# Ending the gathered rows five units earlier, and moving LN2 of the gathered tiles forward

## The reference

```
z = x @ W_in                                   # q, k, v, conv B, C, h and two gates
m = (sigmoid(g_attn) * attention @ W_attn_out + sigmoid(g_conv) * conv @ W_conv_out) @ W_o
h = LN1(2**0.25 * x + m)
q = h @ w_q; per head: top 16 of 128 keys on both halves, top 16 of their 256 sums -> expert, gate
act = gelu(h . u_tab[expert]);  y = sum over 8*16 experts of gate * act * v_tab[expert]
out = LN2(2**0.25 * h + y)
```

## Time and profile before

| | us |
|---|---|
| median of three runs | 3909.4 (3905.04 to 3912.0) |
| the profiled execution | 3916.73 |
| its span, first to last instruction | 3914.9 |
| mean granted clock of PE | 0.985 of full speed |

### The profile page before, as it was taken

How to read it: one execution, slowest core, us unless ns; L and a number is a source line. 1 busy time by engine, 2 the same in 40 slices (tenths; PEclk the granted TensorE clock), 3 DMA queues, 4 the chain that set the end, 5 groups by cost and what they waited for, 6 DMA issues and landing times.

```text
span 3914.9 us, 60806 instructions
## 1 busy us (share of the span) xinstructions
PE 3766.4 (96%) x24471; PEld 3482.9 (89%) x24471; DVE 2720.5 (69%) x3355; ACT 1379.6 (35%) x1966; POOL 1096.0 (28%) x587
## 2 busy tenths in 40 slices
PE   8999999998999999999999889999998888999997
PEld 8999999998988888888888889999998877878785
DVE  4544555455788765566655577888887887888898
ACT  5544444443323100000000334566663333344342
POOL 0000000001634444344433532211113442334442
PEclk9999999999999999999999999999999999999998
DMA  5345555554689999999999449999999999999996
GB/s 186 109 155 182 182 182 182 184 183 169 241 346 384 409 421 399 405 391 408 394 393 391 169 144 354 364 374 376 360 360 396 409 409 376 409 400 393 393 410 243
DMA packets 209849, 1236.87 MB, mean 316 GB/s; under 512 B 20176, under 2 KB 53536, under 8 KB 66336
## 3 DMA queue, kind: packets, MB, share of 16 engines
q1 hardware_dynamic: 124448, 659.65, 44.3%
q0 software_dynamic: 73728, 536.90, 33.6%
q10 hardware_dynamic: 11520, 38.28, 2.4%
HBM read 1196.48 MB, written 37.75 MB: 315 GB/s over the span
## 4 chain that ended last, share of the span: by engine, by line
PE 82%; DMA 9%; DVE 7%; issue 1%; ACT 1%; SPq 0%; ACTq 0%; DVEq 0%
PE dense_ps L909 23%; PE dense_ps L898 13%; PE dense_ps L899 13%; PE dense_ps L900 13%; PE dense_ps L1151 6%; DMA wbuf<-in_peer_v_dram 4%; PE dense_ps L939 3%; PE score_ps L1151 3%; DMA row<-in_peer_v_dram,expert 3%; DVE h L1189 3%; DMA wbuf<-in_w_units_dram 2%; PE o_ps L1151 1%; PE oT_ps L1151 1%; PE score_ps L1108 1%; PE o_ps L1032 1%
## 5 line engine op out<-in xcount | busy, mean ns | idle before, releaser
L1235 DVE TENSOR_TENSOR w_lo<-wbuf,w_hi_r 128x1024 fp32r<-128x1024 f32 x808 | 982.3, 1222 | 575.5 <-ACT w_hi_r L554 575.0
L554 ACT ACTIVATE w_hi_r<-wbuf 128x1024 fp32r<-128x1024 f32 x872 | 915.4, 1059 | 1155.5 <-PE dense_ps L900 631.1
L898 PE MATMUL dense_ps<-act_hi,w_hi_r 128*128 128x256 f32 x4128 | 1185.3, 287 | 49.1 <-DVE w_lo L1235 42.2
L899 PE MATMUL dense_ps<-act_lo,w_hi_r 128*128 128x256 f32 x4128 | 1174.9, 285 | 0.0
L900 PE MATMUL dense_ps<-act_hi,w_lo 128*128 128x256 f32 x4128 | 1174.8, 285 | 0.0
L898 PEld LDWEIGHTS dense_ps<-act_hi,w_hi_r 128*128 128x128 f32 x4128 | 798.9, 194 | 59.8 <-DVE w_lo L1235 34.0
L505 POOL DMA_INDIRECT row<-in_peer_v_dram,expert x256 | 494.6, 1932 | 1127.5 <-DVE h L1189 1103.2
L899 PEld LDWEIGHTS dense_ps<-act_lo,w_hi_r 128*128 128x128 f32 x4128 | 799.0, 194 | 0.0
L900 PEld LDWEIGHTS dense_ps<-act_hi,w_lo 128*128 128x128 f32 x4128 | 798.4, 193 | 0.0
L909 PE MATMUL dense_ps<-xT,wbuf 128*128 128x256 f32 x3136 | 688.1, 380 | 0.8 <-ACT xT L539 0.8
L909 PEld LDWEIGHTS dense_ps<-xT,wbuf 128*128 128x128 f32 x3136 | 594.3, 190 | 86.2 <-issue 5.3
(11 more groups left out here) (220 smaller groups left out, 4214.2 us busy)
## 6 DMA issues: line engine op xcount, KB each, us to landing
wbuf<-in_w_units_dram SPq DMA_DIRECT2D x456, 1024.0 KB
wbuf<-in_peer_v_dram SPq DMA_DIRECT2D x128, 1024.0 KB
act_spill<-stage ACTq DMA_DIRECT2D x64, 256.0 KB, 8.8
gate_spill<-gbuf ACTq DMA_DIRECT2D x8, 2048.0 KB, 11.2
e_act<-act_spill SPq DMA_DIRECT2D x32, 512.0 KB, 10.7
e_gate<-gate_spill SPq DMA_DIRECT2D x32, 512.0 KB, 13.1
cT<-in_x_dram SPq DMA_DIRECT2D x2, 2048.0 KB, 11.3
row<-in_peer_u_dram,expert POOLq DMA_INDIRECT x256
```

Source lines behind the costliest of these rows:

```text
L554: act.activation(w_hi[:, j, :], wbuf[n % 2][:, j, :], ACT.Copy).then_inc(w_hi_ready, 1)
L898: nc.tensor.matmul(out, w[0], x[0], start=opens, stop=False)
L899: nc.tensor.matmul(out, w[0], x[1], start=False, stop=False)
L1235: V.tensor_tensor(w_lo[n % 2][:, j, :], wbuf[n % 2][:, j, :], w_hi[:, j, :].bitcast(F32), ALU.subtract).then_inc(lo_by_dve, 1)
```

## The change

Two numbers of `rows_in` and one line of constants:

```diff
-STATS_AT, SD_AT, APPLY_AT, OUT_AT = (19, 62), (21, 62), (24, 63), (27, 63)
+STATS_AT, SD_AT, APPLY_AT, OUT_AT = (3, 57), (5, 58), (7, 59), (9, 60)
...
     if m >= 0:
         left = ALL_ROWS - ROWS_TO[N_V - 1]
-        return left * min(m + 1, 62) // 62 - left * min(m, 62) // 62
+        return left * min(m + 1, 57) // 57 - left * min(m, 57) // 57
```

## The result

| | before | changed |
|---|---|---|
| median of 20 runs each, us | 3911.73 (3899.76 to 3921.22) | 3919.18 (3914.63 to 3929.91) |
| the profiled execution, us | 3916.73 | 3929.91 |
| its span, us | 3914.9 | 3928.1 |

The ratio is 1.0021 with a 95% interval of 1.0012 to 1.0030, so the change costs 7.5 us by the medians and 8.2 by the ratio (4.7 to 11.7). The profiled execution of the changed kernel is the slowest of its 20, 10.7 us above their median, and the one of the kernel before is 5.0 us above its own; what they show of sizes is read with that in mind.

The account below looks back on a forecast made before the run. It took PE and the nearly full transfers (412 GB/s) as level, with a serial VectorE tail at the end. Terms -6.1 + 0 + 4.2 + 0 - 1.1 = -3.0 us took 3909.4 to 3906.4; range 3897 to 3918.

Parts of the forecast that it names:

- signs of failing: PE ending over 12 us later or earlier at all, 2.52 and 4.71 us waits returning, or a new 5 us wait.
- The tail: At the kernel's end, VectorE starts the last piece at 3883.7 in place of 3889.81: -6.1 us.
- LN2 of tile 1 in its new place: In sections 57 to 59, its 4.7 us of passes fit into VectorE's free time: 0 us, up to +3 without cover.
- The five rows: By section 56, five more rows need 12.7 us of transfers, 3.5 MB in idle capacity: PE ends 4.2 us later.
- rival A: Second table's stage: free capacity is only echo, PE ends 12.7 us later; net +5.5 us, 3914.9; chance 0.20.
- LN2 of tile 0: Moved from sections 19 to 27 to sections 3 to 9: 0 us in sum, between -5 and +5.
- Units 57 to 63: The last units, without rows: the 1.12 us wait at 3833 goes, -1.1 us.

Follow-up runs that it names:

- rows57_ln1: The changed kernel with LN2 of tile 0 back in sections 19 to 27; ratio 1.0017 to the kernel before.
- rows60_ln1: The kernel before with rows ending at unit 59 and LN2 of tile 1 in sections 59 to 62; ratio 1.0003 to the kernel before.
- rows57_only: The kernel before with only the rows moved, ending at unit 56, LN2 of both tiles as before; ratio 1.0020 to the kernel before.
- half-row kernels: Kernel before, changed kernel, and changed kernel with LN2 of tile 0 in sections 19 to 27, each gathering 512 KB from row 408: 0.9908, 0.9904, 0.9893.
- ln0_early: The kernel before with only LN2 of tile 0 moved, to sections 3 to 9; ratio 0.9993 to the kernel before.
- before_half_take: The kernel before with VectorE adding only 1024 of a row's 2048 floats from row 408 on, transfers whole; ratio 0.9968, median 3903.86.

## Why the prediction was wrong

The forecast was 3.0 us faster and the change is 7.5 us slower; 3919.2 lies above the range of 3897 to 3918. Two of the prediction's own signs of failing came: PE's stage was 20.5 us longer in the profile, where 12 was the limit, and the wait of 6.75 us stands before unit 13.

*The tail, -6.1 us:* right to the tenth of a microsecond (19.7 and not 25.8 us behind PE's end), in the changed kernel, in `rows57_ln1` and in `rows60_ln1`.

*LN2 of tile 1 in its new place, 0:* right; PE has no wait after 3840 in the changed kernel.

*The five rows, +4.2 us:* this step failed. The term measured 7.5 + 6.1 = 13.6 us by the medians and 8.2 + 6.1 = 14.3 by the ratio, above my upper bound of 12.7. Its rate was about right (a two-row unit took 11.53 us at 411 GB/s, foreseen 11.45 at 412). Two of its parts were wrong. The count was low: five rows by the issues, but 7.3 MB, seven rows, by the last 65 us, and these would take 17.7 us at 412 GB/s in place of 12.7. And 3.5 MB of them, 8.5 us, were to ride in capacity that lay idle, half of the free capacity that wasn't plain echo, with no row behind the half. In the profiled execution none was used: 398 GB/s before, 399 now. In `rows57_only` and `rows57_ln1` some was, at 403 and 406. From 17.7 and 13.6 I estimate about 4 us used on average, half of what was credited. The two parts, 5.0 and 4.4 us, make up the 9.4 us by which the term was too small. That free capacity behind waits is mostly echo, as rival A had it, is likely and not shown.

*LN2 of tile 0, 0 between -5 and +5:* not contradicted in the full kernel (0.9993 alone, which can't be told finer than 7 us). In the half-row kernels its new place costs some 3 us, so it isn't free where transfers don't bound. The waits of 2.52 and 4.71 us at its old place did not come back there in the changed kernel. But in `ln0_early`, with LN2 of tile 0 gone from there too, 5.29 us stand at 3471, before unit 27, where the 2.52 us had been; that LN2 caused that wait isn't borne out.

*Units 57 to 63, -1.1 us:* the wait is gone; the term is too small to be measured.

So rival A came nearest, with +5.5 us where +7.5 was measured. The nearness is in part luck: its count was low by two rows, and it let no idle capacity be used where some was, and the two errors work against each other. The check that I lacked was the cut 65 us before the end: it asks how many bytes a unit without rows leaves unmoved, 10.88 us less 6.4 us of its own, and needs no guess about usable capacity. As an estimate before the runs it overshoots (five units give 22 us), the count of landed rows undershoots (12.7), and the measured 13.6 lies between.

What stays open: why five row-free units cost 13.6 us and not 22, beyond that the kernel before also had less than full transfers at its end (276 GB/s); how much of the idle capacity denser rows can use, since executions with the same rows show 400 to 406 GB/s; how much of the charge is the lower clock behind additional waits, since no run holds the clock fixed; and how the gain of `before_half_take` divides between late `w_lo` and a better spacing of the gathers.

## What to carry to other kernels

Where a stage has its transfers within a few per cent of full, count bytes before instructions: moving them earlier did not make them free here, and a unit at the end that needs less than its share leaves transfer time unused, most of which was not won back. A cut of the stage at a fixed distance before its end, with GB/s on both sides, gives an upper price for such a move before it is made. Trust no single pair of profiles for its size; here it charged 20.5 us where the medians charge 13.6. Shorten a serial tail only by as much as the bytes that must move ahead of it allow, or take them to a stage that has room first.

## What the runs showed of the hardware

GpSimd working in SBUF on 128x2048 float32 held up VectorE's pass of the same size: 3.76 and 5.47 us where it takes 2.35. The second case reads as if one waited for the other, and not as if both went on at a shared rate. VectorE's pass starts at 3905.63 in the middle of GpSimd's last pass, GpSimd ends at 3908.96, and VectorE ends 2.1 us later, so that hardly anything of its 2.35 us of work was done before. But its pass at 3897.65 took 2.35 us, with GpSimd's second pass from 3898.14 beside it; there VectorE was first, and GpSimd's pass took 6.24 us where its last took 4.50 (spans on GpSimd are rough). The Trainium skill, "SBUF — State Buffer", section "SBUF: two separate sides", says that an instruction of VectorE with two SBUF inputs and one of GpSimd that reads SBUF take a shared pair of ports as a lock for the whole instruction, and whoever comes second waits. These two places agree with that. The pass at 3893.85 does not quite: it ended at 3897.6, before GpSimd's first pass did (3898.07).

The other thing is the rhythm. With two rows in every unit, the changed kernel had from 3716 to 3809 us a fixed period of four units, 46.12 us, at 411 GB/s, with the same three short waits of PE in each (0.73, 0.36 and 0.29 us, then 0.79, 0.39 and 0.28).
